# 64x64 blocks of the recurrence turned two by two, and the gate formed in the channel layout

## The reference

```python
def wkv7_scan(r, w, k, v, a, b, reverse):          # state S: 64x64 for each head
    def step(S, inp):
        r_t, w_t, k_t, v_t, a_t, b_t = inp
        sa = jnp.einsum('bhij,bhj->bhi', S, a_t)
        S = S * w_t[:, :, None, :] + sa[..., None] * b_t[:, :, None, :] + v_t[..., None] * k_t[:, :, None, :]
        return S, jnp.einsum('bhij,bhj->bhi', S, r_t)
    ...

def rwkv7_branch(u, ...):
    ...
    g = jax.nn.sigmoid(xg) @ g_up                    # xg: 128 columns, g: 512
    for d, reverse in enumerate((False, True)):      # two directions
        ...
        wkv = wkv + wkv7_scan(rh, heads(decay), kd, vh, -kk, kk * ah, reverse)
    ...
    y = ((wkv - mean) * lax.rsqrt(var + GN_EPS)).reshape(B, T, RWKV_DIM) * gn_w + gn_b
    y = y + bonus.reshape(B, T, RWKV_DIM).astype(jnp.float32)
    return (y * g).astype(u.dtype)
```

## Time and profile before

| | before |
|---|---|
| runs | 2806.80, 2803.65, 2805.99 us |
| median | 2805.99 us |
| profiled execution | 2804.09 us |
| its span | 2802.3 us |
| TensorE busy | 2696.4 us (96%) |
| VectorE busy | 1570.2 us (56%) |
| ScalarE busy | 926.3 us (33%) |
| mean granted clock of TensorE | 0.994 of full speed |

### The profile page before, as it was taken

One profiled execution on the slowest core, in us unless ns is written; L12 is line 12 of the kernel. 1 busy time (PEld: TensorE's weight loads), 2 busy tenths in 40 slices (PEclk: granted clock), 3 DMA queues, 4 the chain that ended last, 5 costly groups with the idle time before them and its releaser, 6 DMA issues.

```text
span 2802.3 us, 46790 instructions
## 1 busy us (share of the span) xinstructions
PE 2696.4 (96%) x20072; PEld 1996.9 (71%) x20072; DVE 1570.2 (56%) x2947; ACT 926.3 (33%) x1559; POOL 138.3 (5%) x237
## 2 busy tenths in 40 slices
PE   8999999999899999989999999999999999999999
PEld 6878777877643333357777778888877777788887
DVE  5767575766443333355685556665466864633443
ACT  6233333236301000033445542223334455332231
POOL 1010100010000000000000000000000000000000
PEclk9999999999999999999999999999999999999999
DMA  4233333264599999963352336664232532232332
GB/s 159 83 111 118 93 103 119 88 216 157 228 389 427 426 425 426 427 236 92 94 115 104 122 109 186 201 192 133 78 106 79 128 113 98 78 103 98 98 97 76
DMA packets 149990, 471.74 MB, mean 168 GB/s; under 512 B 14640, under 2 KB 41888, under 8 KB 137232
## 3 DMA queue, kind: packets, MB, share of 16 engines
q1 hardware_dynamic: 114720, 367.62, 36.6%
q0 software_dynamic: 24976, 82.71, 9.4%
q10 hardware_dynamic: 10080, 18.35, 2.2%
HBM read 451.05 MB, written 21.51 MB: 169 GB/s over the span
## 4 chain that ended last, share of the span: by engine, by line
PE 81%; DMA 8%; DVE 7%; ACT 3%; issue 1%; SPq 0%; ACTq 0%; POOL 0%; DVEq 0%
PE psum L154 78%; DMA wslot<-in_w_up 3%; DMA wslot<-in_w_gate 3%; PE psum L157 3%; DVE halfL L163 1%; DMA m_in<-in_w_ada 1%; DVE slot L163 1%; DVE X L163 1%; ACT halfH L160 1%; DVE vb L163 0%; DVE n_ht L169 0%; DVE gx L163 0%; DVE hL L169 0%; DVE m_acc L169 0%; DMA X<-in_x 0%
## 5 line engine op out<-in xcount | busy, mean ns | idle before, releaser
L163 DVE TENSOR_TENSOR halfL<-ring,halfH 128x1024 fp32r<-128x1024 f32 x302 | 367.9, 1220 | 531.3 <-ACT halfH L160 530.7
L160 ACT ACTIVATE halfH<-ring 128x1024 fp32r<-128x1024 f32 x302 | 317.2, 1053 | 691.7 <-PE psum L154 689.7
L154 PE MATMUL psum<-hH,halfH 128*128 128x512 f32 x1200 | 482.1, 402 | 1.7 <-DVE hL L169 1.7
L154 PE MATMUL psum<-hH,halfL 128*128 128x512 f32 x1200 | 469.1, 391 | 0.0
L154 PE MATMUL psum<-hL,halfH 128*128 128x512 f32 x1200 | 469.0, 391 | 0.0
L154 PEld LDWEIGHTS psum<-hH,halfH 128*128 128x128 f32 x1200 | 225.7, 188 | 74.8 <-issue 24.2
L154 PEld LDWEIGHTS psum<-hH,halfL 128*128 128x128 f32 x1200 | 225.8, 188 | 48.2
L154 PEld LDWEIGHTS psum<-hL,halfH 128*128 128x128 f32 x1200 | 226.0, 188 | 43.3
L154 PE MATMUL psum<-wslot,XT 128*64 128x512 f32 x1024 | 236.3, 604 | 20.0 <-DMA wslot<-in_w_gate 12.8
L154 PE MATMUL psum<-halfH,hH 128*128 128x512 f32 (+2 forms) x576 | 216.7, 376 | 3.7 <-DVE ks L163 1.8
L154 PE MATMUL psum<-halfL,hH 128*128 128x512 f32 (+2 forms) x576 | 207.2, 360 | 0.0
(11 more groups left out here) (492 smaller groups left out, 4106.3 us busy)
## 6 DMA issues: line engine op xcount, KB each, us to landing
wslot<-in_w_gate SPq DMA_DIRECT2D x32, 2048.0 KB, 25.0
wslot<-in_w_down SPq DMA_DIRECT2D x32, 2048.0 KB, 25.9
ring<-in_w_in SPq DMA_DIRECT2D x120, 512.0 KB, 3.7
wslot<-in_w_up SPq DMA_DIRECT2D x30, 2048.0 KB, 25.9
ring<-in_w_gu SPq DMA_DIRECT2D x88, 512.0 KB, 3.6
m_in<-in_w_ada POOLq DMA_DIRECT2D x96, 256.0 KB, 3.1
m_in<-in_w_ada POOLq DMA_DIRECT2D x48, 512.0 KB, 4.9
ring<-in_w_down SPq DMA_DIRECT2D x44, 512.0 KB, 3.6
```

The lines of the kernel that those rows point to most:

```text
L154: return self.e.matmul(*a, **k)
L160: return self.e.activation(*a, **k)
L163: return self.e.tensor_tensor(*a, **k)
```

## The change

A turn is made of four transposes of 128x128 instead of sixteen products of 64x64. A transpose of 128x128 turns two chunks of both heads at once, and leaves the token of the even or the odd chunk in the partitions and the two heads' channels side by side in the row, where the layout wants heads in the partitions and chunks in the row. So ScalarE's copy out of the bank becomes four copies of 64 partitions x 4 x 64, which put each piece where it belongs (`sorted_out`).

The output is turned before it is gated: `rw_turned` at i = 25, sorted into the free part of US, then the gate as one product of 128x512 with channels in the partitions at i = 27, and VectorE's multiplication there; yH is then made from SBUF, and yL in a new step `low` at i = 28. In the attention the same steps for pair 3 are numbers 11 to 15. The bank of the turned output is released by the sort (`yT`), no longer by yL.

```diff
@@ recurrence_order
-                if pr and i in (25, 27):
-                    yield ("gated", "turned")[(i - 25) // 2], pr - 1
+                if pr and i in (25, 27, 28):
+                    yield {25: "turned", 27: "gated", 28: "low"}[i], pr - 1
@@
-    BETWEEN = {**{1 + i: ("norming", 3, i) for i in range(9)}, 11: ("gated", 3), 12: ("gated_out", 3), 13: ("turned", 3),
-               14: ("turned_out", 3)}
+    BETWEEN = {**{1 + i: ("norming", 3, i) for i in range(9)}, 11: ("turned", 3), 12: ("turned_out", 3), 13: ("gated", 3),
+               14: ("gated_out", 3), 15: ("low", 3)}
@@ TensorE
+        def turned_by_two(o, x):
+            for n in range(0, 512, 128):
+                i = pe.transpose(o[:, n:n + 128], x[:, n:n + 128], ident)
+            return i
@@ rw_values, rw_prep: turned(...) becomes turned_by_two(...), the rest as before
-                turned(bank(b), piece(d, src)).then_inc(*up(f"rw_pe{d}", "pe", pr, d, name))
+                turned_by_two(bank(b), piece(d, src)).then_inc(*up(f"rw_pe{d}", "pe", pr, d, name))
@@ rw_gated, rw_turned
-            for c in range(8):
-                for h in range(2):
-                    i = pe.matmul(bank(b)[HP[h], c * 64:c * 64 + 64], US[:, 13, c * 64:c * 64 + 64],
-                                  gup[:, (2 * pr + h) * 64:(2 * pr + h) * 64 + 64], start=True, stop=True)
-            i.then_inc(*up("rw_pe", "gate", pr))
+            pe.matmul(bank(b), gup[:, pr * 128:pr * 128 + 128], US[:, 13, :], start=True,
+                      stop=True).then_inc(*up("rw_pe", "gate", pr))
@@
-            pe.wait_ge(*at("Y_gated", pr))
-            turned(bank(b), US[:, pr, :]).then_inc(*up("rw_pe", "y_turned", pr))
-            free[b] = [("yL", pr)]
+            pe.wait_ge(*at("Y_sum", pr))
+            turned_by_two(bank(b), US[:, pr, :]).then_inc(*up("rw_pe", "y_turned", pr))
+            free[b] = [("yT", pr)]
@@ ScalarE
+        def sorted_out(o, b):
+
+            to, of = o.rearrange("p (n c x) -> p n c x", c=2, x=64), b.rearrange("p (n h x) -> p n h x", h=2, x=64)
+            for c in range(2):
+                for h in range(2):
+                    i = ac.activation(to[HP[h], :, c, :], of[HP[c], :, h, :], COPY)
+            return i
@@ rw_values, rw_prep (i = 5, 6, 7)
-            ac.activation(Vn[pr % 2], bank(ADA_BANK), COPY).then_inc(*up("rw_act", "Vn", pr))
+            sorted_out(Vn[pr % 2], bank(ADA_BANK)).then_inc(*up("rw_act", "Vn", pr))
@@
-            ac.activation(yH[pr], bank(CHAIN_BANKS[1][1]), COPY).then_inc(*up("rw_act", "yH", pr))
+            sorted_out(US[:, 4 + pr, :], bank(CHAIN_BANKS[1][1])).then_inc(*up("rw_act", "yT", pr))
+
+        def rw_gated(pr):
+            ac.wait_ge(*at("Y_gated", pr))
+            ac.activation(yH[pr], US[:, pr, :], COPY).then_inc(*up("rw_act", "yH", pr))
@@ VectorE
-            ve.wait_ge(*at("Y_sum", pr))
-            ve.tensor_tensor(US[:, pr, :], US[:, pr, :], bank(CHAIN_BANKS[0][1]), M).then_inc(*up(R_, "Y_gated", pr))
-
-        def rw_turned(pr):
+            ve.wait_ge(*at("yT", pr))
+            ve.tensor_tensor(US[:, pr, :], US[:, 4 + pr, :], bank(CHAIN_BANKS[0][1]), M).then_inc(*up(R_, "Y_gated", pr))
+
+        def rw_low(pr):
             ve.wait_ge(*at("yH", pr))
-            ve.tensor_tensor(yL[pr], bank(CHAIN_BANKS[1][1]), yH[pr].bitcast(F32), SU).then_inc(*up(R_, "yL", pr))
+            ve.tensor_tensor(yL[pr], US[:, pr, :], yH[pr].bitcast(F32), SU).then_inc(*up(R_, "yL", pr))
```

More of the change, by code:

```diff
@@ L1062, in rw_values @@
             pe.wait_ge(*at("us", 8 + pr))
-            turned(bank(b), US[:, 8 + pr, :]).then_inc(*up("rw_pe", "v_turned", pr))
+            turned_by_two(bank(b), US[:, 8 + pr, :]).then_inc(*up("rw_pe", "v_turned", pr))
             free[b] = [("Vn", pr)]
@@ L1764, in rw_prep @@
                 ac.wait_ge(*at("pe", pr, d, name))
-                ac.activation(piece(d, name), bank(CHAIN_BANKS[d][i % 2]),
-                              COPY).then_inc(*up(f"rw_act{d}", "ev", pr, d, name))
+                sorted_out(piece(d, name), bank(CHAIN_BANKS[d][i % 2])).then_inc(*up(f"rw_act{d}", "ev", pr, d, name))
             elif i >= 14 and PRODS[i - 14][0] in BY_ACT:
@@ L2058, in scalar_program @@
         handlers = {"rkv": rkv_tile, "U": rkv_out, "x": x_ready, "tables": tables, "kk": rw_kk, "lora": rw_lora, "values": rw_values, "early": rw_early, "prep": rw_prep,
-                    "turned": rw_turned, "gemm": rw_gemm, "spill": rw_spill, "ms": a1_ms, "turn": a1_turn,
+                    "turned": rw_turned, "gated": rw_gated, "gemm": rw_gemm, "spill": rw_spill, "ms": a1_ms, "turn": a1_turn,
                     "norming": rw_norming}
@@ L2096, in a1_finish @@
             ac.activation(oH[hp], oF1, COPY).then_inc(*up("at_act", "a1", "oH", ("g", hp)))
-        del handlers["turned"]
+        del handlers["turned"], handlers["gated"]
         handlers |= {"exp": a1_exp, "turn1": a1_turn1, "joint_out": a1_joint_out, "less": a1_shrink,
-                     "spread_out": a1_spread_out, "keep": a1_keep, "finish": a1_finish, "turned_out": rw_turned}
+                     "spread_out": a1_spread_out, "keep": a1_keep, "finish": a1_finish, "turned_out": rw_turned, "gated_out": rw_gated}
         for step, *args in attention1_order():
@@ L3030, in vector_program @@
         handlers = {"rkv": rkv_tile, "tables": tables, "shift": shifted, "kk": rw_kk, "early": rw_early, "begin": rw_begin, "prep": rw_prep, "bonus": rw_bonus,
-                    "loop": rw_loop, "norming": rw_norming, "gated": rw_gated, "turned": rw_turned, "ada": rw_ada, "mods_out": rw_mods_out,
+                    "loop": rw_loop, "norming": rw_norming, "gated": rw_gated, "low": rw_low, "ada": rw_ada, "mods_out": rw_mods_out,
                     "gemm": rw_gemm, "sum": a1_sum, "ms": a1_ms, "scale": a1_scale, "gain": a1_gain, "rope": a1_rope_}
@@ L3092, in a1_finish @@
             ve.tensor_tensor(oL[hp], oF1, oH[hp].bitcast(F32), SU).then_inc(*up(D1, "a1", "oL", ("g", hp)))
-        del handlers["gated"], handlers["turned"]
+        del handlers["gated"]
         handlers |= {"fill": a1_fill, "permute_out": a1_permute_out, "less": a1_less, "factors": a1_factors, "spread_out": a1_spread_out,
-                     "finish": a1_finish, "gated_out": rw_gated, "turned_out": rw_turned}
+                     "finish": a1_finish, "gated_out": rw_gated}
         for step, *args in attention1_order():
```

## The result

The changed kernel takes 2815.57 us (median of 9 runs, 2809.92 to 2818.23) against 2806.07 for the kernel before (9 runs, 2802.20 to 2809.56): ratio 1.0034, 95% interval 1.0025 to 1.0043. It is 9.5 us slower; 7 faster was forecast. The profiled execution took 2816.09 us.

A forecast was written before the change was run, and what follows sets the result against it. TensorE, busy 96% of the span and 81% of the chain, was taken as the bound. Place by place: +0.1 - 0.3 - 1.9 - 1.8 - 0.7 - 2.5 + 0 = -7.1 us, median 2798.9, 8-in-10 range 2793 to 2804.

The forecast's parts named there:

- The price of a sort: ScalarE's four copies of 64x256 replacing one eviction: 1.22 us, 1.12 until the next work, 0.62 more than now.
- Rival 3: A 64-partition copy costs as much as 512 columns, 2.1 us a sort; 16 sorts on the path, net +8, 2814; chance 0.05.
- a wait near 100.7, one of about 2.1 us before the U GEMM: TensorE's expected new waits in the first pair, at i = 6 and i = 7; first pair's sum +0.1 us.
- the sum itself: Place-by-place total from the first pair to the first attention: -7.1 us, giving a median of 2798.9.
- the third and fourth pair: Preparation at i = 5 to 7: savings of 0.5 and 1.35 pass through, -1.9 and -1.8 us.
- the three outputs: Outputs of pairs 0 to 2, at i = 25 and 27: -0.7, -0.9 and -0.9 us.
- rival 1: VectorE and ScalarE hold back the third and fourth pair like the second: 0.3 each, -4.0, time 2802; chance 0.26.
- The first pair: Preparation at i = 5 to 7: +0.1 at i = 5, 6; +0.8 less 0.85 at i = 7; sum +0.1 us.
- The third loop: Values turn there: sort starts 0.54 earlier and lasts 0.62 longer, on the chain to TensorE's wait at 487.06: 0.
- the attention: Pair 3's output in the first attention: 1.5 gained at the gate, later waits balance it by 648.80: 0.
- Rival 4: The weights' stream absorbs the saving if the queue since 665 sets the transfers: time stays 2806; chance 0.05.
- TensorE's price of a turn: Four full transposes, 0.44 us instead of 1.28: about 0.85 saved alone, 1.35 for two together, 2.3 for four.

The follow-up runs named there:

- kept-busy kernels: Transposes of the identity put in TensorE's waits: on the changed kernel, 2808.44 us, ratio 1.0012; on the changed kernel with three-piece sorts, 2797.97 us, ratio 0.9973.
- a sort of 1.15 us: Changed kernel with each sort in three pieces, two of 64 partitions and one of 128, crossing of half the data left out: 2802.31 us, ratio 0.9993.
- the filling: Changed kernel with three-piece sorts, plus transposes of the identity in TensorE's remaining waits: 2797.97 us, ratio 0.9973 to the kernel before.
- the uncrossed one: Changed kernel with each of a sort's four pieces read from the same partition half that it is written to: 2813.41 us, single execution.
- the reordered one: Changed kernel with the four pieces in another order, the two staying in their partition half first, then the two crossing: 2810.13 us, single execution.
- experiment 10: Changed kernel with two of the four pieces of each of the preparation's 24 sorts on VectorE: 2817.65 us against 2805.96.

## Why the prediction was wrong, by its steps

**The price of a sort failed.** "Four: 3 x 0.28 + 0.38 = 1.22 us, and 1.12 until the next work begins" took the 0.27 between copies of 128 partitions for pieces of 64. They last 0.38 as in the prediction, and start 0.39 apart: 1.56, in the 32 sorts alike. The prediction had named a sort of 1.5 us or more as a sign that it is wrong. The figure of the Trainium skill cited there (ScalarE: Activation LUTs, What ACT_TABLE_LOAD costs; measured there on a tile of 128 partitions, and for 256 columns an estimate of 0.40 for a copy with 0.09 of overlap) agrees in the duration with the 0.38 here; the overlap is there behind pieces of 128 partitions (0.10) and not behind these. What the kernel pays for it, an estimate from two runs: the kept-busy kernels with sorts of 1.56 and 1.15 us stand 2.1 us over and 5.8 under their own before, 7.9 us for 0.41 us of sort, as if 19 of the 32 sorts lay on the path. Rival 3 had counted 16.

**The clock was missing altogether.** The prediction read "a wait near 100.7, one of about 2.1 us before the U GEMM" and priced each wait at its own length. The waits came, at 101.56, at 103.13 and, 4.19 us long, before the U products, and around and behind them TensorE ran at 1.2 GHz. Filling the waits gives 7.1 us back. So the account is: -7.1 forecast, +7.9 for the sort's price, +7.1 for the clock, +7.9 in all, where 9.5 was measured. The 1.6 left are within the noise: each of these differences of medians has an interval of 2.5 to 4 us either way. For the same reason the sum itself, at its own price and without the clock, can't be told from right: it said 7.1, where 5.8 was measured, with an interval of 4.5 to 10.7 by the ratio. One of its readings is off without changing a term: of the 1.95 us from the old gate to the product behind it, 0.79 is waiting and not 1.0.

**The places.** At a sort of 1.15 us the third and fourth pair give 2.0 each, for 1.9 and 1.8 forecast, and the three outputs 3.0 for 2.5: the reading of who waits there was right, and rival 1, which let those pairs give 0.3 each, was not. The first pair's +1.3 for +0.1 is the clock again (1.7 us lost in one stretch); with the filling it is -0.2. At 1.56 us a sort the pairs' savings are eaten in the row of four turns at i = 5, 6, where the third turn waits for the first's sort: 1.20 and 0.91 us in the third pair (table: +0.8, with one lowered clock in it). The third loop was called 0 on the ground that the sort starts 0.54 earlier and lasts 0.62 longer; it lasts 1.06 longer than the copy, and its wait is 2.03 us for 1.13, with two lowered clocks near it. In the attention, also called 0, the transposes wait 2.35 us for the sort at 657.81, again with the clock down behind. The wait is the same in the trace of the outputs' part alone.

**Rival 3** had the sign, the place and the mechanism, "a 64-partition copy [...] costs as much as 512 columns", with the point from which it decides at 1.65 us a sort. The sort came at 1.56 us, below it; the clock made the rest. Its 0.05 was too little: of its two ends for the price (0.6 and 2.1) the prediction used one inside, on a row of another shape, and gave the upper end almost no weight. Rival 4 is not supported: behind the attention the changed kernel does gain 4.1 us of the 16.1 in that one execution, but others lose up to 1.8 there, and the runs' medians carry 9.5 to the end.

**Right:** TensorE's price of a turn (0.35 to 0.45 us from its start to the next product forecast; 0.35 ahead of a large product, 0.44 in a row of turns, and 0.59 in the loops, where 64x64 products follow), ScalarE's +31 us (32.5), that no wait on TensorE ends with yH or yL, and, as far as the noise allows, the outputs' 2.5 (2.6 measured alone).

## What to carry to other kernels

A wait on TensorE has two prices: its length, and the clock of what comes behind. Where a change adds waits, look at the granted clock of the stretches behind, and test with harmless products in the wait. Copies that are cut into pieces are to be priced from a row with the same number of partitions, columns and source; where no row has them, the price is a range, and its upper end deserves weight. Before moving work to an idle engine, ask who waits for a bank it holds: ScalarE was busy 32% of the window before and 37% after, and still set the time. And one trace is one execution: two of these kernels with the same sorts and first waits were 6 us apart at the same instruction, counted from the start of the first pair.

## What was not expected of the hardware

- Copies out of PSUM on ScalarE of 256 columns let the next start 0.28 us later when they have 128 partitions and 0.39 when they have 64, crossed or not and in both orders tried, whatever the next one has; one lasts 0.38 in both cases.
- The same waits do not always lower the clock: behind first waits of 1.77 and 0.92 us it was halved for 6.8 us in the changed kernel (from 102.3), for 3.4 in the uncrossed one (from 100.7) and not at all in the reordered one, and the three stood 14.7, 7.2 and 6.4 us behind at the same later instruction. The two ends of the changed kernel's clock show it in the time: 2809.92 us at 0.992, 2816.09 at 0.989.
- On VectorE four pieces of 64 partitions and 256 columns out of PSUM take 1.77 us, 0.43 each (experiment 10).
